# Half of the key-value memory keeps two gate pieces from pass 2 to pass 4, keys laid out by pairs of chunks, and one load of p's weights serves chunks 6 and 7

## The reference

```
for i in range(2):
    h = rmsnorm(x, mix_norm[i])
    if i == 0:  x = x + pool_mixer(h, pool_w[0], pool_scale[0])
    else:       k_nope, k_pe, v = shared_kv(x, ...)
                x = x + mla_mixer(h, ..., k_nope, k_pe, v, cos, sin)      # causal attention, 8 heads
    x = x + peer_mixer(rmsnorm(x, ffn_norm[i]), peer_wq[i], peer_keys[i], peer_u[i], peer_v[i])
    g = sigmoid(rmsnorm(x, ple_norm[i]) @ ple_wg[i])                     # the gate
    x = x + g * (p[i] @ ple_wp[i])                                       # "p's weights" are ple_wp
return rmsnorm(x, final_norm)
```

## Time and profile before

| | |
|---|---|
| median of 3 runs | 2887.83 us (2886.12 to 2888.53) |
| the profiled execution: its time, its span | 2894.77 us, 2893.0 us |
| granted PE clock, mean | 0.905 of full |
| busy: PE, DVE, ACT, POOL | 79%, 74%, 37%, 44% of the span |
| DMA | 406 GB/s over the span |
| loads by SP of 1024 KB | 78, the keys of the experts among them, plus 12 of 768 KB |

### The profile page before, as it was taken

One profiled execution on the slowest core, in us unless ns is written; L12 is line 12 of the kernel. 1 busy time (PEld: TensorE's weight loads), 2 busy tenths in 40 slices (PEclk: granted clock), 3 DMA queues, 4 the chain that ended last, 5 costly groups with the idle time before them and its releaser, 6 DMA issues.

```text
span 2893.0 us, 23323 instructions
## 1 busy us (share of the span) xinstructions
PE 2281.1 (79%) x6572; PEld 1176.2 (41%) x6572; DVE 2142.1 (74%) x4486; ACT 1072.7 (37%) x3181; POOL 1278.6 (44%) x1029
## 2 busy tenths in 40 slices
PE   6787777977879987888687999799967788766555
PEld 4444233522534543455253455346624333222112
DVE  6877768885797667757979766676696788677776
ACT  2433324333244433632324443364332244333222
POOL 2353543454443444444433344444344344555652
PEclk8999988998999998999899999899989899987777
DMA  8999999999999999999999999999999999999995
GB/s 357 416 386 419 413 420 397 409 420 420 420 383 411 420 420 420 419 420 420 395 420 394 418 410 419 420 400 398 420 392 420 419 387 415 419 420 420 420 420 234
DMA packets 164787, 1175.37 MB, mean 406 GB/s; under 512 B 18481, under 2 KB 19889, under 8 KB 23601
## 3 DMA queue, kind: packets, MB, share of 16 engines
q0 software_dynamic: 147456, 1073.81, 90.4%
q1 hardware_dynamic: 16624, 98.24, 8.3%
q10 hardware_dynamic: 576, 1.84, 0.2%
HBM read 1171.71 MB, written 2.10 MB: 406 GB/s over the span
## 4 chain that ended last, share of the span: by engine, by line
PE 35%; DMA 34%; DVE 19%; ACT 5%; issue 4%; POOL 2%; DVEq 0%; SPq 0%; ACTq 0%; POOLq 0%
DMA slot<-in_uv,idx 34%; PE acc L931 19%; DVE slot L1638 7%; DVE X L1629 2%; PE B L685 2%; PE M L603 2%; PE B L603 2%; PE M L873 2%; POOL slot L580 2%; PE M L685 1%; ACT diag L1156 1%; PE B L873 1%; ACT w L1150 1%; DVE SD L1266 1%; DVE top_u L1271 1%
## 5 line engine op out<-in xcount | busy, mean ns | idle before, releaser
L931 PE MATMUL acc<-slot,diag 128*128 128x512 f32 x2904 | 1558.1, 677 | 576.8 <-ACT diag L1156 575.3
L580 POOL DMA_INDIRECT slot<-in_uv,idx x1024 | 1278.3, 1248 | 1571.9 <-PE acc L931 1106.0
L1638 DVE CUSTOM_DVE_ANT_0 slot<-slot,HP 128x1024 f32<-128x1024 f32 x1024 | 1244.1, 1221 | 602.6 <-DMA slot<-in_uv,idx 593.1
L931 PEld LDWEIGHTS acc<-slot,diag 128*128 128x128 f32 x2904 | 575.0, 210 | 1416.9 <-ACT diag L1156 846.0
L1148 ACT ACTIVATE act_a<-a 128x1 f32<-128x1 f32 x1024 | 206.7, 202 | 1629.7 <-DVE a L1638 1628.6
L1629 DVE SCALAR_TENSOR_TENSOR X<-slot,w,X 128x1024 f32<-128x1024 f32 x297 | 380.6, 1282 | 24.0 <-ACT w L1150 23.9
L1150 ACT ACTIVATE w<-act_a,gate 128x1 f32<-128x1 f32 x1024 | 301.7, 295 | 33.2
L1156 ACT ACTIVATE diag<-cst,w 128x128 f32<-128x128 f32 x726 | 291.5, 402 | 23.8
L685 PE MATMUL B<-TT,w 128*128 128x256 f32 (+1 forms) x448 | 88.0, 351 | 0.0
L685 PE MATMUL M<-TT,w 128*128 128x256 f32 (+1 forms) x448 | 87.3, 349 | 0.0
L685 PEld LDWEIGHTS B<-TT,w 128*128 128x128 f32 x448 | 77.3, 193 | 20.6 <-issue 13.0
(11 more groups left out here) (201 smaller groups left out, 1559.9 us busy)
## 6 DMA issues: line engine op xcount, KB each, us to landing
w<-in_wq SPq DMA_DIRECT2D x28, 1024.0 KB, 9.1
slot<-in_uv,idx POOLq DMA_INDIRECT x1024, 14.3
w<-in_ple_wg SPq DMA_DIRECT2D x8, 1024.0 KB, 9.0
w<-in_w_o SPq DMA_DIRECT2D x8, 1024.0 KB, 9.2
w<-in_w_dq SPq DMA_DIRECT2D x6, 1024.0 KB, 9.5
w<-in_w_uq_nope SPq DMA_DIRECT2D x8, 768.0 KB, 8.5
w<-in_ple_wp SPq DMA_DIRECT2D x5, 1024.0 KB, 10.5
slot<-in_wq SPq DMA_DIRECT2D x4, 1024.0 KB, 15.6
```

Source lines behind the costliest of these rows:

```text
L580: nc.gpsimd.indirect_dma_start(out=slot[s][:], out_offset=None, in_=uv[g // NC], in_offset=bass.IndirectOffsetOnAxis(ap=idx[:, g % HPB, k: ...
L931: last = nc.tensor.matmul(acc[:, half * 512:half * 512 + 512], diag[adds_on_pe(n) % DIAGS][:], slot[s][:, D + half * 512:D + half * 512 + ...
L1638: nc.vector.tensor_tensor_reduce(out=slot[s][:, 0:D], in0=slot[s][:, 0:D], in1=HP[:, g % HPB, :], scale=1.0, scalar=0.0, op0=ALU.mult, op1 ...
```

## The change

Three edits. First, KT is laid out by pairs of chunks, so that keys and values of chunks 0 and 1 take up places 0 and 2 of KV, and those of chunks 2 and 3 take up places 1 and 3. Places 1 and 3 are thus free until the second `keys` stage, and hold pieces 0 and 1 of layer 0's `ple_wg` from `gates(0, 2)` (in pass 2) to `gates(2, 2)` (in pass 4). Second, a score is cut at the pair's border: 384 columns become 256 + 128, and 512 become 256 + 256, for KT and for KPE. Third, the stage `wp(7)` and its load are gone, and `add(6)` computes both chunks.

```diff
-    residual(6) + embed(6, 1) + stages_of(["wp"], 7, 1),
+    residual(6) + embed(6, 1),
...
-KEPT = [("wq", (1, 2)), ("ple_wg", (4, 6, 7))]
+KEPT = {**{("wq", g, i): ((1, 2), i) for g in (1, 2) for i in range(4)},
+        **{("ple_wg", g, i): ((0, 2), 2 * i + 1) for g in (0, 2) for i in range(2)},
+        **{("ple_wg", g, i): ((4, 6, 7), i) for g in (4, 6, 7) for i in range(4)}}
...
+        elif (name, g0, i) in KEPT:
+            groups, at = KEPT[name, g0, i]
+            there = g0 != groups[0]
+            if not there:
+                loads[at] += 1
+            found.append(("KV", at, loads[at] - 1, held[at], there))
+            held[at] = n
...
-        KT = KV[:, 0:NC * D].rearrange("p (h s) -> p h s", h=H)
+        KT = KV[:, 0:NC * D].rearrange("p (q h s) -> p q h s", q=2, h=H)
...
-                if where == "ring" and had is not None:
+                if where in ("ring", "KV") and had is not None and not there:
                     sp.wait_ge(weights_used, had + 1)
...
-                        dst, h = B[:, e * 512:e * 512 + width], 2 * k + e
-                        nc.tensor.matmul(dst, QT[:, h, q0:q0 + P], KT[:, h, 0:width], start=True, stop=False)
-                        last = nc.tensor.matmul(dst, QPT[:, h, q0:q0 + P], KPE[:, 0:width], start=False, stop=True)
+                        h = 2 * k + e
+                        for q in range(c // 2 + 1):
+                            at, cols = q * W2, min(width - q * W2, W2)
+                            dst = B[:, e * 512 + at:e * 512 + at + cols]
+                            nc.tensor.matmul(dst, QT[:, h, q0:q0 + P], KT[:, q, h, 0:cols], start=True, stop=False)
+                            last = nc.tensor.matmul(dst, QPT[:, h, q0:q0 + P], KPE[:, at:at + cols],
+                                                    start=False, stop=True)
...
             def add_stage(g0, n):
                 pe.wait_ge(pt_loaded, 16 * (EMBED_GROUPS.index(g0) + 1))
-                wait_mb("add", g0, n)
+                last_two = g0 == PAIRS - 2
+                wait_mb("add", g0, n + last_two)
                 wp = piece("ple_wp", g0, 0)
-                for i in range(n):
+                for i in range(n + last_two):
```

More of the change, by code:

```diff
@@ L175 @@
         "asks0": [("wq", [0, 1, 2, 3])], "asks1": [("wq", [4, 5, 6, 7])], "gates": [("ple_wg", [0, 1, 2, 3])],
-        "add": [("ple_wp", [0])], "wp": [("ple_wp", [0])], "tail": [("ple_wg", [0, 1, 2, 3])]}
+        "add": [("ple_wp", [0])], "tail": [("ple_wg", [0, 1, 2, 3])]}
 PARTS = {
@@ L195 @@
     "add": lambda g, n: [5 * n, 4, 1, 1],
-    "wp": lambda g, n: [5, 1],
     "tail": lambda g, n: [1, 0],
@@ L242 @@
 AT, TOTAL = totals()
-EMBED_GROUPS = [g0 for s, g0, n in SCHEDULE if s in ("add", "wp")]
+EMBED_GROUPS = [g0 for s, g0, n in SCHEDULE if s == "add"]
 KEY_GROUPS = [g0 for i, (s, g0, n) in enumerate(SCHEDULE) if s == "asks0" and (g0 == 0 or any(
@@ L268 @@
 FIRST_SLOT = SLOTS - FIRST_PIECES
-KEPT = [("wq", (1, 2)), ("ple_wg", (4, 6, 7))]
+KEPT = {**{("wq", g, i): ((1, 2), i) for g in (1, 2) for i in range(4)},
+        **{("ple_wg", g, i): ((0, 2), 2 * i + 1) for g in (0, 2) for i in range(2)},
+        **{("ple_wg", g, i): ((4, 6, 7), i) for g in (4, 6, 7) for i in range(4)}}
 def homes():
-    found, ringed, first = [], [], {}
+    found, ringed, loads, held = [], [], [0] * 4, [None] * 4
     for (name, g0, i), n in PIECES.items():
-        kept = [(k, groups) for k, (kept_name, groups) in enumerate(KEPT)
-                if name == kept_name and g0 in groups and i < 4]
         if n < FIRST_PIECES:
             found.append(("slot", FIRST_SLOT + n, 0, None, False))
-        elif kept:
-            k, groups = kept[0]
-            found.append(("KV", i, k, None, g0 != groups[0]))
+        elif (name, g0, i) in KEPT:
[5 more added lines that the diff above has]
+            held[at] = n
         else:
@@ L528, in _ @@
                 if name == "ple_wp":
-                    width, c = size.get(("add", g0), 1) * P, g0 % NC
+                    width, c = (size["add", g0] + (g0 == PAIRS - 2)) * P, g0 % NC
                     if groups:
@@ L534, in _ @@
                 where, h, loads, had, there = HOMES[n]
-                if where == "ring" and had is not None:
+                if where in ("ring", "KV") and had is not None and not there:
                     sp.wait_ge(weights_used, had + 1)
-                if where == "KV" and not there and i == 0:
-                    next_ffn = NC + 2 if name == "ple_wg" else g0
-                    sp.wait_ge(x_ready, before("x_ready", "fnorm", next_ffn))
+                if where == "KV" and not there and i == 0 and g0 in (1, NC):
+                    sp.wait_ge(x_ready, before("x_ready", "fnorm", NC + 2 if name == "ple_wg" else g0))
                 if not there:
@@ L876, in half_product @@
                 return last
[L878 to L888, removed]
             def tail_stage(g0, n):
@@ L918, in _ @@
                           dq=dq_stage, uq=uq_stage, uqp=uqp_stage, heads=heads_stage, wo=wo_stage,
-                          enorm=enorm_stage, gates=gates_stage, add=add_stage, wp=wp_stage, tail=tail_stage)
+                          enorm=enorm_stage, gates=gates_stage, add=add_stage, tail=tail_stage)
             def gather(n):
@@ L1017, in keys_stage @@
                 for i in range(2):
-                    nc.scalar.activation(KT[:, 4 * i:4 * i + 4, c * P:(c + 2) * P], MB[i][:, :].rearrange(blocks, t=W2),
+                    nc.scalar.activation(KT[:, c // 2, 4 * i:4 * i + 4, :], MB[i][:, :].rearrange(blocks, t=W2),
                                          ACT.Copy).then_inc(copied[i], 1)
```

## The result

The changed kernel takes 2900.11 us (median of 16 runs, 2892.27 to 2902.43); the kernel before 2888.86 us (16 runs, 2885.17 to 2895.08). The medians lie 11.3 us apart, where +8.2 was forecast. The ratio on record, for which all the runs are used, is 1.003, which is +8.7 us; its 95% interval, 1.0022 to 1.0039, is +6.4 to +11.3 us. So the change is slower, and the forecast lies inside the interval. The profiled execution took 2899.89 us, span 2898.1, granted clock 0.905.

The account below looks back on a forecast made before the run. The DMA at 420 GB/s was taken to set the pace in most slices, DVE or PE in some stretches. +5.0 - 0.6 + 0 + 5.8 - 2.0 = +8.2 us on the median of 2887.83 gave 2896.0 us, range 2884.5 to 2900.

Parts of the forecast that it names:

- The pace, and the burst: Pass 2: two gate loads move to 762 us, where the DMA sets the pace, costing +5.0 us.
- DVE's last wait for a row: Sign in pass 2: the last wait before DVE's full stretch comes at about 807 in place of 802.1 us.
- The 0.6 us given back: Pass 2, gate products from 860 to 900 us: at most -0.6 us comes back at the loads' old place.
- Pass 4's loads: Pass 4: two gate loads vanish where PE is late, not the rows; 0 us, bounds 0 and -5.0.
- The rival by bytes: Whole kernel: each MB saved is time saved, three loads -7.5, scores +5.8, so 2886.1 us; 14 in 100.
- The scores: Attention of pass 5: cut scores take longer by 0.21 us per added matmul switch, +0.84 or +0.82 us each.
- The term "+5.8": Attention of pass 5: the cut scores' cost on the path, +2.5 in group 6 and +3.3 in group 7.
- that edge: Attention of pass 5: one score runs at 1.2 GHz, raising the scores' upper bound from 6.6 to 7.4 us.
- POOL's waits: Sign in pass 5: POOL's waits around 1897 and 1950 us grow by 1 to 2 us each.
- p's weights: Last pass: one load less where DVE waits for rows, -2.0 us, bounds -2.5 and +1.
- The new wait of DVE: Last pass: DVE waits some 4 us at its product with the gate until PE has made B's product too.
- the 0.5 charged for them: Last pass: 0.5 us charged for gathers issued later by DVE's waits, against the -2.5 us of the load.

Follow-up runs that it names:

- rotary_first: The changed kernel with another order in a score: the rotary product whole first, then the keys in two halves; 2894.5 us, ratio 1.0018.
- no_keep: The changed kernel without the two kept gate pieces, which go through the ring in passes 2 and 4 as before; 2898.4 us, ratio 1.0039.
- cut_only: The kernel before with the scores cut at 256 columns and nothing else; 2898.51 us, ratio 1.0035.
- wp_only: The kernel before with one load of p's weights for both last chunks and nothing else; 2885.35 us, ratio 0.9991.
- cut_keys_only: The kernel before with only the keys' product cut at 256 columns, the rotary product whole and first; 2893.31 us, ratio 1.0009.
- keep_late: The changed kernel keeping gate pieces 2 and 3 instead of 0 and 1, requested only after 0 and 1 are used; 2901.5 us, ratio 1.0046.
- burst_four: The kernel before, same bytes, with all four gate pieces of pass 2 loaded into KV right behind the last query pieces; 2900.1 us, ratio 1.0038.
- timed: The kernel before, same bytes, with the gate weights of passes 2, 4 and 6 requested later, through one more wait on SP; 2879.65 us, ratio 0.9972.
- timed_wp: The kernel before with gate weights of passes 2, 4 and 6 requested later, and one load of p's weights for both last chunks; 2878.13 us, ratio 0.9968.

## Why the prediction was right, and where it was off

**The pace, and the burst: right.** +5.0 was forecast for two loads moved to 762, and the lag's step is +5.0 (and +5.0 again in rotary_first, +10.5 for four loads). Pass 2 began 4.7 us earlier in this execution than in that of before, and at dot product 280, the one at 805.19, it is 0.3 us later: the 5.0 us came in between. DVE's last wait for a row stands there, one dot product further on than the one at 802.12:

```profile
794.93 1.22 DVE L1633 CUSTOM_DVE_ANT_0 slot<-slot,HP 128x1024 f32<-128x1024 f32 x1 [1.01 <-DMA slot<-in_uv,idx]
...
805.19 1.22 DVE L1633 CUSTOM_DVE_ANT_0 slot<-slot,HP 128x1024 f32<-128x1024 f32 x1 [0.56 <-DMA slot<-in_uv,idx]
```

What the kept pieces cost in a mean execution the medians tell poorly. Three pairs give it: the changed kernel less no_keep, +1.0; the changed kernel less cut_only and wp_only together, +3.6; rotary_first less cut_keys_only and wp_only together, +5.7. Forecast were 4.4, keep_late speaks against it, and doubled the term stands in burst_four's median.

**The 0.6 us given back: not seen.** The rest of pass 2 has +0.5 in the changed kernel, within the scatter. Pass 2 came out 5.5 us longer, where 4.4 was forecast.

**Pass 4's loads: right.** 0 was forecast and -0.1 measured in this trace, with PE gapless and DVE waiting for PE's product 1.6 us in place of 0.7. The rival by bytes fell twice over: burst_four and timed have the same bytes and lie 20.5 us apart.

**The scores: right mechanism, a size too small.** The starts are 0.63 and 0.42 us apart, as worked out. PE's timeline in group 6's first two scores:

```profile
1870.19 0.49 PE L813 MATMUL B<-KV,TU 128*128 128x128 f32 x2
1870.61 0.49 PE L814 MATMUL B<-KPE,A 64*128 64x128 f32 x2
1871.03 0.70 PE L813 MATMUL B<-KV,TU 128*128 128x256 f32 x2
1871.65 0.70 PE L814 MATMUL B<-KPE,A 64*128 64x256 f32 x2
...
1876.17 0.70 PE L813 MATMUL B<-KV,TU 128*128 128x256 f32 x2 [1.07 <-ACT SC L1061]
...
1878.26 1.18 PE L813 MATMUL B<-KV,TU 128*128 128x256 f32 x2
1879.36 1.22 PE L814 MATMUL B<-KPE,A 64*128 64x256 f32 x2
1880.51 0.79 PE L813 MATMUL B<-KV,TU 128*128 128x128 f32 x2
```

The term "+5.8" was the sum of these lengths at 2.4 GHz, with one score at the lower clock held for an edge. In this trace that edge is the case, and twice: from 1878.26 on the starts are 1.1 us apart in place of 0.63, and again from 1939.69. The granted clock shows it:

```profile
1870.00:1890.00 20.00, 18.93 (x61) 10.01 (x59) 14.64 (x26) 12.37 (x31) 7.04 (x6) 0.83 0.86 344
1930.00:1950.00 20.00, 18.45 (x40) 7.99 (x41) 13.90 (x23) 10.83 (x23) 4.12 (x4) 0.74 0.92 382
```

and in the kernel before, with its two scores that come behind a wait:

```profile
1870.00:1890.00 20.00, 18.93 (x54) 8.04 (x53) 16.44 (x28) 13.67 (x36) 8.01 (x6) 1.00 1.01 407
1930.00:1950.00 20.00, 18.44 (x45) 7.05 (x44) 16.01 (x28) 12.77 (x33) 5.89 (x4) 0.83 0.94 377
```

```profile
1876.77 0.91 PE L808 MATMUL B<-KV,TU 128*128 128x384 f32 x2 [1.07 <-ACT SC L1066]
...
1932.94 1.12 PE L808 MATMUL B<-KV,TU 128*128 128x512 f32 x2 [1.56 <-ACT SC L1066]
...
1937.17 2.07 PE L809 MATMUL B<-KPE,A 64*128 64x512 f32 x2
```

So before has a score at the lower clock too, near 1937 us. The two stretches from which the prediction took "1.00 and 0.98" all but leave it out. PE's timeline tells what each part costs, by the distance from the start of one score to that of the next (worked out from the timelines, us):

```
                           group 6, scores        group 7, scores
                         1-2    2-3    3-4      1-2    2-3    3-4
before                   6.32   8.24  12.91     7.65  12.79  12.94
timed_wp (scores uncut)  6.31   8.24  12.91     7.65   9.54  12.94
after (the change)       7.13  12.24  13.72     8.46  15.18  13.74
```

Where all are at the full clock a score costs 0.80 to 0.82 us more: the switches, as forecast. In the other two, which hold the lower clock, the changed kernel is 4.0 and 2.4 us longer than before; that is 3.2 and 1.6 us beyond the switches, and against timed_wp, all of it at the full clock, 3.2 and 4.8. Over these six distances the switches make 4.9 us and the lower clock 4.8 us more than in before. The prediction had the switches right and the clock at nothing.

Over the whole stretch, 1870 to 2000 us, changed kernel and before:

```profile
1870.00:2000.00 130.00, 126.65 (x486) 72.08 (x485) 90.00 (x148) 74.03 (x184) 59.14 (x47) 0.93 0.93 371
1870.00:2000.00 130.00, 124.92 (x456) 66.62 (x455) 96.01 (x155) 77.61 (x197) 64.61 (x50) 0.97 0.98 396
```

The granted clock is 0.93 in each of the four kernels that alternate, and 0.95 to 1.00 in the eight others, before among them; the GB/s are 365 to 376 against 390 to 413. The difference of 25 GB/s over 130 us is 7.7 us of the DMA, and the lag grows by 8.0. What brings the lower clock about? The waits for the exponential alone don't: they have the same length (1.07 us in group 6 and 1.55 in group 7) in all the traces, 0.2 us more in the two with the rotary product first. Behind them all four alternating kernels go over to the lower clock at both places. Of the other eight one does so in group 6 (cut_keys_only), and four in group 7 (before, burst_four, timed, rotary_first). The alternation goes with the lower clock, then, but one execution each doesn't show how often an uncut kernel has it.

POOL's waits grew less than forecast at the first place and as forecast at the second. Its timeline for the earlier trace rows:

```profile
1894.74 1.42 POOL L582 DMA_INDIRECT slot<-in_uv,idx  x1 [4.10 <-PE acc L926]
...
1949.44 1.03 POOL L582 DMA_INDIRECT slot<-in_uv,idx  x1 [11.23 <-PE acc L926]
...
1973.91 1.68 POOL L582 DMA_INDIRECT slot<-in_uv,idx  x1 [5.48 <-PE acc L926]
```

That is +0.6, +1.9 and +0.9 us. The term measured +8.0 in this trace, 7.8 as the mean of four; against the mean of the eight kernels that don't alternate it is 9.5, and cut_only's medians give +10.4.

On the Trainium skill ("TensorE: Matmul & The Clock Gate", section "Step-by-step: what each phase is for"): the next tile's weights load under the matmul that runs. Where both matmuls have 128 rows the trace agrees (the two halves of the keys in rotary_first take 0.85 us, where one whole takes 0.84); between 128 and 64 rows it doesn't, by 0.21 us each.

**p's weights: right, some 0.7 us too cautious.** The last pass in the timelines of PE and DVE:

```profile
2610.92 4.24 PE L605 MATMUL M<-w,pt 128*128 128x512 f32 x8
...
2616.71 3.60 PE L605 MATMUL B<-w,pt 128*128 128x512 f32 x8
```

```profile
2620.35 1.22 DVE L1547 TENSOR_TENSOR A<-A,M 128x1024 f32<-128x1024 f32 x1 [4.56 <-PE B L605]
...
2630.58 0.16 DVE L1176 RECIPROCAL rstd<-rms 128x1 f32<-128x1 f32 x1 [3.24 <-ACT rms L944]
```

The new wait of DVE is there (4.56 us, some 4 forecast), and the wait for ACT behind it is 3.24 us as before. The eight buffers covered both: the step is -2.9 us here, -2.7 in the mean of the seven kernels with one load and by wp_only's medians, so the 0.5 charged for them wasn't due.

**The sum.** Counted from the start of pass 2, pass 5 ends 11.7 us later than before, where 10 were forecast. By the changed kernel's trace the terms are +5.0, +0.5, -0.1, +8.0 and -2.9: +10.5, beside +8.2 forecast, +11.3 by the medians and +8.7 by the ratio. The step that was off is the term "+5.8" of the scores: it took the clock as full and measured +8.0 to +10.4, 2.2 to 4.6 us more. The 0.6 given back and p's weights are smaller errors, and p's has the opposite sign. The time came out 4.1 us above the forecast of 2896.0, just beyond the range's end of 2900.0; 1.0 of it is that before stood at 2888.86 here. That the sum fits better than its largest term is in part luck.

## What to carry to other kernels

Find the stretches in which the DMA is full and those in which it idles behind an engine, before counting bytes: a load in the first costs its whole transfer (2.5 us for 1 MiB here), in the second little or nothing, until the idle time there is used up. That idle time (missing GB/s times the stretch) is an estimate of what a rearrangement can win there; the gains here, 3.3 of 6.5 us and 4.2 to 4.8 of 5.9, stayed below it. Memory that frees a buffer earlier also lets the queue run ahead, so a kept weight can make the next loads come at a worse time; holding a request back by one wait on the right signal won 0.3% with no byte saved. When a tiled operand must be cut, keep matmuls of like rows next to each other: cut with alternating rows the scores cost 10.4 us, with like rows together 4.0 or less.

## What the runs showed of the hardware that was not expected

- In float32, a change between a matmul of 128 rows and one of 64 rows costs 0.21 us each time, at 128, 256, 384 and 512 columns; a cut between matmuls of like rows costs 0.01 us in the rows of rotary_first.
- The same wait of PE (1.07 us, and 1.55 us) was followed by the lower clock (starts 1.1 us apart in place of 0.63, 1.2 in place of 2.4 GHz) in both places in all four kernels that alternate, and in 5 of 16 such places in the others.
- Executions of one unchanged program part by several microseconds. In the heads, the uncut kernels that went over to the lower clock in group 7 lie at 0 (before), -2.0, +1.0 and +4.5 us, and those that didn't at -2.0 to -5.5. So a profile of a single execution can end 5 us before its neighbour while the median is 4 us above it, as with cut_keys_only, where the trace of before lies 5.5 us above the median of before in that comparison.
